# ScalarE makes one affine pass a chunk after each norm; VectorE and 512-column ScalarE passes form the high parts

## What is computed

```python
def rms_norm(x, gain):
    xf = x.astype(jnp.float32)
    inv = lax.rsqrt(jnp.mean(xf * xf, axis=-1, keepdims=True) + EPS)
    return (xf * inv).astype(x.dtype) * gain

def first_block(...):
    ...
    for i in range(DEPTH):
        ...
        h = rms_norm(x, norm_g[i, 1]) * (1.0 + sc2) + sh2
        x = x + g2 * peer_ffn(h, peer_w_q[i], peer_keys[i], peer_u[i], peer_v[i])
    return rms_norm(x, final_g)

def second_block(...):
    ...
        h = layer_norm(DEEPNORM_ALPHA * h + mix, ln_g[layer, 0], ln_b[layer, 0])
        ffn = conv_ffn(h, ffn_w_up[layer], ffn_conv_w[layer], ffn_conv_b[layer], ffn_w_down[layer])
        h = layer_norm(DEEPNORM_ALPHA * h + ffn, ln_g[layer, 1], ln_b[layer, 1])
```

## Time and profile before

| | |
|---|---|
| median of 3 runs | 3089.91 us (3087.83 to 3095.05) |
| span of the profiled execution | 3087.6 us (the page gives no other time for it) |
| mean granted TensorE clock | 0.967 |
| TensorE busy with matmuls | 2940.5 us, 95% |
| VectorE busy | 2234.2 us, 72% |
| ScalarE busy | 1632.8 us, 53% |
| mean HBM traffic | 162 GB/s |

### The profile page before, as it was taken

How to read it: one execution, slowest core, us unless ns; L and a number is a source line. 1 busy time by engine, 2 the same in 40 slices (tenths; PEclk the granted TensorE clock), 3 DMA queues, 4 the chain that set the end, 5 groups by cost and what they waited for, 6 DMA issues and landing times.

```text
span 3087.6 us, 57563 instructions
## 1 busy us (share of the span) xinstructions
PE 2940.5 (95%) x19494; PEld 2680.6 (87%) x19494; DVE 2234.2 (72%) x4764; ACT 1632.8 (53%) x3372; POOL 62.4 (2%) x112
## 2 busy tenths in 40 slices
PE   7998899999999999999999999999999999898898
PEld 6887899999887778899999988887898889797896
DVE  5336499888779984649888877776585578655786
ACT  1112557778544443655777854444554257463674
POOL 3000000000001100000000000000000000000000
PEclk8999999999999999999999999999999999997999
DMA  9521455444478853445444455555441145442453
GB/s 385 192 89 36 137 189 170 152 162 141 157 255 311 309 197 112 147 150 187 160 154 158 144 170 190 188 188 182 140 134 52 55 164 174 143 137 69 144 169 122
DMA packets 137685, 502.97 MB, mean 163 GB/s; under 512 B 15312, under 2 KB 15440, under 8 KB 137264
## 3 DMA queue, kind: packets, MB, share of 16 engines
q1 hardware_dynamic: 122544, 445.57, 42.5%
q0 software_dynamic: 14976, 55.19, 4.9%
HBM read 498.60 MB, written 2.10 MB: 162 GB/s over the span
## 4 chain that ended last, share of the span: by engine, by line
PE 81%; DVE 5%; ACT 4%; issue 1%; DVEq 0%; ACTq 0%
PE PB L535 14%; PE PB L536 14%; PE PB L537 14%; PE PA L577 9%; PE PA L579 9%; PE PA L578 9%; PE PA L760 4%; PE PB L525 2%; DVE w_low L2204 1%; PE PA L969 1%; PE PA L1141 1%; PE PA L620 1%; PE PA L648 1%; ACT h_high L1283 1%; ACT w_high L1180 1%
## 5 line engine op out<-in xcount | busy, mean ns | idle before, releaser
L1180 ACT ACTIVATE w_high<-ring 128x512 fp32r<-128x512 f32 x1548 | 961.7, 629 | 854.4 <-PE PA L579 466.7
L2204 DVE TENSOR_TENSOR w_low<-ring,w_high 128x512 fp32r<-128x512 f32 x1548 | 1050.6, 690 | 437.0 <-ACT w_high L1180 422.3
L535 PE MATMUL PB<-h_high,w_low 128*128 128x256 f32 x3792 | 1098.8, 290 | 45.5 <-DVE h_low L1870 36.3
L536 PE MATMUL PB<-h_low,w_high 128*128 128x256 f32 x3792 | 1076.4, 284 | 0.0
L537 PE MATMUL PB<-h_high,w_high 128*128 128x256 f32 x3792 | 1075.5, 284 | 0.0
L535 PEld LDWEIGHTS PB<-h_high,w_low 128*128 128x128 f32 x3792 | 736.9, 194 | 63.8 <-issue 45.8
L536 PEld LDWEIGHTS PB<-h_low,w_high 128*128 128x128 f32 x3792 | 724.8, 191 | 0.0
L537 PEld LDWEIGHTS PB<-h_high,w_high 128*128 128x128 f32 x3792 | 724.3, 191 | 0.0
L577 PE MATMUL PA<-w_low,a_high 128*128 128x512 f32 x1200 | 475.2, 396 | 11.1 <-DVE a_low L2213 10.6
L579 PE MATMUL PA<-w_high,a_high 128*128 128x512 f32 x1200 | 473.4, 395 | 0.0
L578 PE MATMUL PA<-w_high,a_low 128*128 128x512 f32 x1200 | 472.8, 394 | 0.0
(11 more groups left out here) (330 smaller groups left out, 2564.0 us busy)
## 6 DMA issues: line engine op xcount, KB each, us to landing
ring<-tiles SPq DMA_DIRECT2D x842, 512.0 KB, 3.3
BIG<-ada POOLq DMA_DIRECT2D x96, 512.0 KB, 6.7
BIG<-skew POOLq DMA_DIRECT2D x4, 512.0 KB, 4.3
X<-x SPq DMA_DIRECT2D x1, 1024.0 KB, 6.0
skew<-BIG POOLq DMA_DIRECT2D x1, 1024.0 KB, 7.7
out<-X SPq DMA_DIRECT2D x4, 256.0 KB, 2.0
con<-consts SPq DMA_DIRECT2D x1, 853.0 KB, 8.9
BIG<-masks POOLq DMA_DIRECT2D x1, 768.0 KB, 6.4
```

The source lines that it names most:

```text
L535: mm(dst, lhs_l, high, start=start, stop=False, skip_group_check=True)
L536: mm(dst, lhs_h, low, start=False, stop=False, skip_group_check=True)
L1180: fn(tile_half(w_high, s, b), ring[:, at:at + HALF], ACT.Identity).then_inc(sem("high_ready"), 1)
L2204: tt(tile_half(w_low, s, b), ring[:, at:at + HALF], tile_half(w_high, s, b).bitcast(F32), ALU.subtract).then_inc(sem("low_ready"), 1)
```

## The change

`affine` makes one pass a chunk, in place. For the first two of the four pairs (`HIGH_BY_ACT = 2`) VectorE now copies the result into `h_high` and then subtracts. For the other two ScalarE waits for its own signal of the pair and copies 512 columns into `h_high`, which signals `pair_high`; VectorE waits for that and subtracts. VectorE handles pair 0 before the fourth scaling product, and the other pairs after it. The parts have the same values as before.

```diff
--- before.py
+++ after.py
@@ -298,6 +298,7 @@
         LOW_MASKS = way_masks[:, 0:PAIR_LEVELS * P]
 
         SUMS = ["experts0", "experts1", "down0", "down1"]
+        HIGH_BY_ACT = 2
 
         def added(name, m):
 
@@ -1279,11 +1280,13 @@
                         act.wait_ge(sem("scaled"), w.up(sem("scaled")))
                     dk, g = dst[:, m * T:(m + 1) * T], gain[:, m:m + 1]
                     add = {} if shift is None else {"bias": shift[:, m:m + 1]}
-                    if split:
-                        fn(h_high[:, m * T:(m + 1) * T], dk, ACT.Identity, scale=g, **add)
                     ins = fn(dk, dk, ACT.Identity, scale=g, **add)
                     if m % 2:
                         ins.then_inc(sem(name), 1)
+                        w.up(sem(name))
+                        if split and m // 2 >= HIGH_BY_ACT:
+                            act.wait_ge(sem(name), w.value(sem(name)))
+                            fn(two(h_high, m // 2), two(dst, m // 2), ACT.Identity).then_inc(sem("pair_high"), 1)
 
             def norm_affine(i, split=True):
                 affine(X, p("ln_g", i * DC, DC), p("ln_b", i * DC, DC), "x_out", split)
@@ -1856,36 +1859,44 @@
                 ins.then_inc(sem("mod_ready"), 1)
                 dve.wait_ge(sem("mod_ready"), w.up(sem("mod_ready")))
 
-            def scale(dst):
+            def scale(dst, name=None):
 
                 dve.wait_ge(sem("root_ready"), w.up(sem("root_ready")))
                 v.reciprocal(inv[:, :], inv[:, :]).then_inc(sem("dve_step"), 1)
                 dve.wait_ge(sem("dve_step"), w.up(sem("dve_step")))
                 for i in range(DC // 2):
+                    if i == DC // 2 - 1 and name is not None:
+                        split_fresh(dst, name, 0)
                     tt(chunks(two(dst, i)), chunks(two(X, i)), over(inv[:, :], 2), ALU.mult)\
                         .then_inc(sem("scaled"), 1)
+                if name is not None:
+                    for i in range(1, DC // 2):
+                        split_fresh(dst, name, i)
 
             def split_pair(src, name, i):
                 dve.wait_ge(sem(name), w.up(sem(name)))
                 tt(two(h_low, i), two(src, i), two(h_high, i).bitcast(F32), ALU.subtract)\
                     .then_inc(sem("h_split"), 1)
 
-            def split_whole(src, name):
-                for i in range(DC // 2):
-                    split_pair(src, name, i)
-
-            def split_x():
-                split_whole(X, "x_out")
-
-            def rms(name, dst, run=None):
+            def split_fresh(src, name, i):
+
+                dve.wait_ge(sem(name), w.up(sem(name)))
+                if i < HIGH_BY_ACT:
+                    v.tensor_copy(two(h_high, i), two(src, i)).then_inc(sem("dve_step"), 1)
+                    dve.wait_ge(sem("dve_step"), w.up(sem("dve_step")))
+                else:
+                    dve.wait_ge(sem("pair_high"), w.up(sem("pair_high")))
+                tt(two(h_low, i), two(src, i), two(h_high, i).bitcast(F32), ALU.subtract)\
+                    .then_inc(sem("h_split"), 1)
+
+            def rms(name, dst, run=None, split=None):
                 if name is not None:
                     dve.wait_ge(*added(name, DC - 1))
                 if run is not None:
                     split_low(run, 0)
                 w.up(sem("squares_ready"), DC // 2)
-                scale(dst)
+                scale(dst, split)
                 if run is not None:
-                    split_whole(dst, "whole_ready")
                     split_low(run, 1)
 
             def layer_norm(i, name, run=None):
@@ -1900,9 +1911,7 @@
                     split_low(run, 1)
                 dve.wait_ge(sem("centered"), w.up(sem("centered"), DC // 2))
                 w.up(sem("squares_ready"), DC // 2)
-                scale(X)
-                if run is not None:
-                    split_x()
+                scale(X, "x_out" if run is not None else None)
 
             def inverse_heads(n):
                 dve.wait_ge(sem("head_roots"), w.up(sem("head_roots")))
@@ -2567,7 +2576,7 @@
             gated_heads(HG_MIX, HG_HEADS, lambda h: p("hg_norm_g", h, 1), HG_G)
             scale_heads(HG_MIX, HG_HEADS)
             add_product("hg_out", modulation(0, 0, 2))
-            rms("hg_out", HB, "wq0")
+            rms("hg_out", HB, "wq0", "whole_ready")
             peer(0)
             rms("experts0", H)
             modulate(LATER + 2, LATER + 4, PB[:, 1024:])
@@ -2644,11 +2653,10 @@
             split_low("lru_out", 1)
             modulate(LATER + 4, 12, PA[:, 1024:])
             add_product("lru_out", modulation(1, 0, 2))
-            rms("lru_out", HB, "wq1")
+            rms("lru_out", HB, "wq1", "whole_ready")
             peer(1)
             split_low("even_in", 0)
-            rms("experts1", X)
-            split_x()
+            rms("experts1", X, split="x_out")
             split_low("even_in", 1)
             even_mixer()
             layer_norm(0, "even_out", "up0")
```

## The result

The changed kernel took 3071.24 us (median of 4 runs, 3064.90 to 3076.16) against 3089.15 us before; the ratio is 0.9937, 95% interval 0.9921 to 0.9953. In a later comparison of five runs with 21 of before it was 3070.22 to 3089.13, ratio 0.9936 (0.9923 to 0.9950). So the change is worth about 18 to 20 us, 0.6%. Direction and place are right, the size is a third too small.

What follows compares the result with a forecast made beforehand. TensorE held 81% of the chain, waiting at six norms on ScalarE's pace; wq0 2.4, wq1 2.6, up0 2.9, odd_in 3.4, up1 1.3 and even_in 0.2 sum to 12.8: 3089.9 - 12.8 = 3077.1 us, range 3072 to 3086.

Steps and rivals of the forecast that it cites:

- The place: At six norms (wq0, wq1, even_in, up0, odd_in, up1) TensorE waits for `h_low`, and ScalarE's pace ends last.
- The timetable: From S, a norm's first scaling start: `h_low` passes near S+2.3, 4.0, 4.6, 6.1; TensorE's first matmul at S+3.15, not 3.67.
- the hidden fourth scaling: VectorE's fourth scaling ends only at S+3.64; ScalarE wants it at S+4.34, so the delay costs nothing.
- Rival 2: VectorE becomes the gate: its copy takes 0.69 us, costing up to 0.5 us a site, 3 in all; 3080 us, chance 0.08.
- rival 3: The saving is absorbed by the second tile or ScalarE's own-semaphore wait: 0 to 3 us, 3088 us, chance 0.06.
- Where TensorE turns dense: At sites with shifts TensorE never runs dry from S+4.84 on, against S+9.47 before: 4.6 us earlier.
- The clock's rise at S+9.0: TensorE's clock rises to 2.4 GHz at S+9.0, from a range of S+7.2 to S+9.5; at wq0 before, about S+11.8.
- Rival 1: The clock rises as long after the first matmul as before, 0.5 us earlier only: saves 7.9 us, 3082 us, chance 0.22.
- even_in at 0.2: The norm even_in, without shifts, already feeds TensorE nearly fast enough, so it saves only 0.2 us.
- Nothing charged elsewhere: After the first tile, the split of tile 2 on ScalarE and VectorE also comes earlier, so no cost was charged.
- The sum at the last rise in time: With the clock rising at S+7.2, the six norms give 3.1, 3.4, 3.6, 4.1, 2.0 and 0.6: 16.8 us.
- Rival 4: Slower: the clock stays low longer behind the norms, rising 4 us later than before, S+15.8 at wq0; 3096 us, chance 0.05.

Runs made afterwards that it cites:

- the second experiment: The changed kernel with `HIGH_BY_ACT = 0`, so ScalarE makes all four high parts and VectorE copies none: 3083.90 us, ratio 0.9986 to the kernel before.
- the halves: The change at up0, odd_in and up1 only: 3079.58 us, ratio 0.9973; at wq0, wq1 and even_in only: 3084.92 us, 0.9990; both against the kernel before.

## Why the prediction was right or wrong

- **The place** was right: ScalarE's pace at six norms, read from the waits and the timeline. TensorE's wait fell as forecast.
- **The timetable** was right to 0.1 us on all three engines, the copy at 0.42 and the hidden fourth scaling too. Rival 2 (VectorE as the gate) and rival 3 (absorbed) are refuted.
- **Where TensorE turns dense** was right: S+4.7, no pause after.
- **The clock's rise at S+9.0** failed. It was taken toward the late end of S+7.2 to S+9.5, on the grounds of the two busiest sites. It came at S+8.1 (wq0), about 9.1 (wq1), 6.4 (up0) and 6.8 (up1); at up0 and up1 earlier than the early end. wq0 was worth 2.9 us and not 2.4, up0 4.0 and not 2.9, up1 2.5 and not 1.3. At odd_in the gate matmuls ran at the high clock from further forward: 4.0 instead of 3.4. What failed is the step "lag after TensorE turned dense, added to S+4.84": the rise has no fixed lag from there. With the same code at up0 it came at S+6.4, 6.3 and 6.3 in three traces (the changed kernel twice, and all copies on VectorE) and at S+9.6 with the layer norms alone changed; with the old code at up1 at S+7.3 in the kernel before and at S+13.4 with the other norms alone changed. Rival 1, by which the rise keeps its lag behind the first matmul, fails too: at wq0 that lag was 8.1 us before and is 4.9 now. Only at up1 did the rise move by about the 0.5 us of that rival. The budget of time that the Trainium skill ("TensorE: Matmul & The Clock Gate", Part 1) speaks of can't be counted from the first matmul where pauses follow it.
- **even_in at 0.2** failed: 1.6. The sum looked at the first tile only. The 32 narrow matmuls behind it start 0.9 us earlier from S (8.26 against 9.13), which the pauses and a rise 0.3 us earlier give, and take 4.2 us instead of 5.0, because less of them is at the low clock.
- **Nothing charged elsewhere** is open. The sum and its range held only the six norms. These alone came to 17.7 us, 4.9 more than the forecast 12.8: about 3.5 by the clock's rises and 1.4 at even_in. That is the greater part of the miss; behind the norms low stretches came (3 and 1 us at even_in) and went (at up1), and the 1 to 2 us by which the 19 to 20 exceed the six norms are within the spread. So it isn't shown that this term failed. The sum at the last rise in time, 16.8 us, was the nearest to what came, and the range went 1 us beyond it.
- Rival 4 (slower, by the clock) didn't come: at none of the norms did the clock rise later. That arrival and clock together can cost more than the timetable says shows in the second experiment, where pairs that start 0.2 to 0.5 us later at wq0 go with 14 us.

Two things stay open. One is how much of the 19.8 us is stretches far from the norms: the times of the halves say 5 to 8, with an uncertainty as large, the counts at the norms say 2. The other is what sets the moment of the rise, and why the clock falls at 2198 in one kernel and not in the other; the traces with the same code at up0 and different rises show that the norm's own timetable alone doesn't.

## What to carry to other kernels

Where a matmul engine starves between short bursts behind a norm, time each producer's instructions from the norm's start and lay out the new timetable: it can be right to a tenth of a microsecond. Price the clock separately, and as a range: here the path was worth 2.5 us a norm and the clock 0 to 2 more, and with the same code at a norm the rise came 3 and 6 us apart. Allow a few microseconds either way for low stretches elsewhere, even in a kernel with one edit, and don't read a cause from one profile.

## What the runs showed of the hardware

- Keeping TensorE busy through a norm, with starved pairs behind, kept the clock at 1.00 for all 14 us at up0 and up1, but only to S+8.2 at wq0, S+5.5 at wq1 and S+5.7 at odd_in; the kernel was 4 us slower. With dense pairs behind, it held at all four, and the time was that of the changed kernel without it.
- The mean granted clock goes with the kernel: 0.967 on average in 21 runs of before (0.964 to 0.968), 0.971 in five with the change (0.970 to 0.973), with some 3 us of time for each 0.001 within one kernel.
- The same code at a norm saw the clock rise at different times: S+6.4 and S+9.6 at up0 (changed kernel, layer norms alone changed), S+7.3 and S+13.4 at up1 (kernel before, the other norms alone changed).
- VectorE's copy of 512 columns from fp32 to fp32r, SBUF to SBUF, took 0.42 us against 0.69 for the subtraction of 512.
